# A hybrid decoder layer on one core: the router at four items a head, gates from item 53, 34 more rows in the U half, and a mixer end that adds squares

## The chip, the cores and the metric

One Trainium2 chip, one of its cores. The time is device microseconds (us) of one execution of the whole program; lower is better. The engines are TensorE (PE), VectorE (DVE), ScalarE (ACT), GpSimd (POOL) and SyncE (SP); SP issues most transfers, POOL the indirect ones.

## The reference

One layer over 512 prompt tokens and 32 sample tokens (T = 544), width 1024. What the change touches:

```python
h = h + concat([y_ssd, y_lru]) @ w_out          # the mixer's end, 16 output products
xn = rmsnorm(h, norm_ffn)
q = (xn @ wq).reshape(n, 8 heads, 2 halves, 128)
s_top, i_top = top_k(einsum(q, sub_keys), 16)    # 2 x 128 keys a head
best, pos = top_k(sums of the pairs, 16)         # 16 of 16384 experts a head
g = softmax(best)
act = gelu(einsum(xn, expert_u[idx]))
h = h + einsum(g * act, expert_v[idx])
```

Then a gated embedding and a last rmsnorm. All in float32.

## The kernel before, in words

The program has three stages: the mixer, the experts and the closing. Each engine's instructions are written out in one order; only semaphores tie the engines.

**Mixer.** 51 weight tiles, n = 0 to 50, one product of 48 matmuls each. The last eight (from OS0 = 43) belong to the residual. ssd_add(d) on DVE adds the product to h through tmp, ACT squares h[d] into one of two buffers sq, and PE sums the squares over the partitions with a matmul by ones, sums(3, d). The root of the sum starts the experts' norm. Ahead of that SP spreads rows of decays: the L tiles (1 MB each) and ce (spread_e), which carry(c) on DVE waits for.

**Experts.** 384 prompt tokens (the last three blocks of 128) are dense: all 16384 experts are computed and a gate matrix of 128 x 128 per token masks them. The other 128 prompt tokens and the 32 sample tokens are sparse: their 320 rows of experts are gathered one index per partition, 160 of U (a dot product each) and 160 of V (an addition each).

The order is by items. Items 0 to 143 are the U half: 16 of them are query items (QITEM, 48 matmuls, two per head), 128 are U items (24 matmuls, then a gelu into one of four buffers Ab, which SP stores to acts). Items 144 to 271 are the V half (24 matmuls each). Every item takes a weight tile from a ring of four: SP loads Rw, ACT casts it to Rh, DVE makes the rest Rl. In step n the engines do: PE product n; ACT the evacuation of n, then the cast for n + 4, which waits for product n's end; DVE Rl(n + 4), then its other work of step n; SP, eight ahead, the act store of n and the load of n + 8.

The other work is placed by numbers. A head that starts at item n has its scores behind item n + 3, and topk in six parts from step n + 5 on DVE. After four heads (a group) come, from LOOK[g]: decode, five look-ups (lookup(g, 0) is the sparse prompt block, 1 to 3 the dense ones, in every second step, and lookup(g, NDB) the samples), and softmax in step LOOK[g] + 9. The sparse two and softmax free 80 indices for the gathers (idx); sx tells PE that the dense tokens' numbers (gs) are there. At TURN PE transposes them, turns(). From G0 to GEND 96 gate units stand between the items: one-hot tiles on DVE and ACT, four matmuls on PE, a copy into stg on ACT, and a store of gates by SP for every eight units.

ROWS says how many sparse rows are done by which item; between its points rows are spread evenly. row(r) waits for its gather; POOL has four buffers ug for the gathers.

At GEND SP waits until all gates have landed, then loads Gq (1.5 MB, gates of eight expert rows) and three Aq (acts of four rows, 0.75 MB each). DVE multiplies them (h_full), ACT casts the product to Hh, DVE makes Hl, and item 144 can start. h_hi(0) stands behind the evacuation of item 143 on ACT. In V a new Aq comes every four items and a new Gq every eight, ahead of the next Rw on SP's queue.

Of the kernel before, what the change touches and what calls it, by code (L numbers as in the profile page):

```python
# [9 lines left out]
ALU = mybir.AluOpType  # L10
# [24 lines left out]
NIT = 2 * PH + PK  # L35
HEAD_AT = [0, 6, 12, 18, 34, 40, 46, 52]
LOOK = [29, 63]
QITEM = [n + 2 * s for n in HEAD_AT for s in range(2)]
# [134 lines left out]
def mixer(nc, sh, ring, x, wm, par, head, w_rg, w_ig, conv_in, s0, lru0, ssd_p, ssd_s, conv_o, lru_o):  # L173
# [71 lines left out]
    tmp = at("tmp", A6, [P, T])  # L245
    rstdB = at("rstdB", A6 + 2 * T * 4, [P, T])
    yh = at("yh", A4, [P, ND, T], F32R)
    yl = at("yl", A5, [P, ND, T], F32R)
# [15 lines left out]
    def sync(sp):  # L264
# [8 lines left out]
        def spread_e(c):  # L273
            for g in range(NG):
                spread(ce[g * 64:g * 64 + 64, c % 2, :, :].rearrange("p j l -> p (j l)"),
                       eacd[c, g * HG:(g + 1) * HG, :].rearrange("j l -> (j l)"), 64, "ce%d" % (c // 3))

# [8 lines left out]
        for n in range(2, NW):  # L286
# [26 lines left out]

            if n == 38:
                sp.wait_ge(S("mm"), OL0)
                for c in range(2, 4):
                    spread(L[c][:, :, :].rearrange("p h l -> p (h l)"), acsd[c, :, :].rearrange("h l -> (h l)"), P,
                           "ab%d" % (c // 2))
                sp.wait_ge(S("act_c"), 2 * NXC)
                sp.wait_ge(S("cout_s"), 2 * NXC)  # L320
                spread_e(1)
                spread_e(2)
                sp.dma_start(conv_o, cout[:, :, :]).then_inc(S("out_s"), 16)
# [92 lines left out]
    def tensor(pe):  # L416
# [172 lines left out]
        for n in range(NW):  # L589
# [31 lines left out]
            if n == OS0:  # L621
                pe.wait_ge(S("sad"), 5)
                pe.wait_ge(S("shl"), 3 * ND)
                for k in range(ND):
                    sums(2, k, sq8[:, k, :])
            if n >= OS0 + 2:
                d = n - OS0 - 2
                if d == 0:
                    pe.wait_ge(S("root"), 3)
                sums(3, d, sq[:, d % 2, :])  # L630
        for d in range(ND - 2, ND):
            sums(3, d, sq[:, d % 2, :])

    def scalar(a):
# [88 lines left out]
        for n in range(1, NW + 1):  # L723
# [129 lines left out]
            if n >= OS0 + 2:  # L853
                d = n - OS0 - 2
                a.wait_ge(S("ose"), 2 * (d + 1))
                if d >= 2:
                    a.wait_ge(S("sq_free"), 3 * ND + d - 1)
                square(3, d, sq[:, d % 2, :], h[:, d, :])
        a.wait_ge(S("ose"), 2 * ND)
        a.wait_ge(S("sq_free"), 4 * ND - 2)  # L860
        square(3, ND - 1, sq[:, (ND - 1) % 2, :], h[:, ND - 1, :])
        ring.hi(a, 3)

    def vector(v):
# [109 lines left out]
        def carry(c):  # L974
            v.wait_ge(S("ce%d" % (c // 3)), 64 if c < 3 else 32)
            v.tensor_copy(dec[:, c, :], ce[:, c % 2, :, P - 1:P].rearrange("p j a -> p (j a)")).then_inc(S("cem"), 1)
            v.wait_ge(S("cem"), 2 * c - 1)
            v.tensor_tensor(ce[:, c % 2, :, :], ce[:, c % 2, :, :],
                            xs[:, 9:10, chunk(c)].broadcast_to([P, HG, P]), ALU.mult).then_inc(S("cem"), 1)
# [35 lines left out]
        def ssd_lo(k, part):  # L1015
# [3 lines left out]
            else:  # L1019
                v.wait_ge(S("shl"), 2 * ND + k + 1)  # L1020
                v.wait_ge(S("sq_ready"), 3 * ND)
            v.scalar_tensor_tensor(out=yl[:, k, t], in0=xs[:, k, t], scalar=col("norm_ssd", k),
                                   in1=yh[:, k, t].bitcast(F32), op0=ALU.mult, op1=ALU.subtract).then_inc(S("sll"), 1)

        def sample_add(b):
# [15 lines left out]
        for n in range(1, NW + 1):  # L1041
# [188 lines left out]
            if n >= OS0 + 1:  # L1230
                ssd_add(n - OS0 - 1)
            if n == NW - 1:
                for m in range(3):
                    ring.lo(v, m)
        ring.lo(v, 3)

# [3 lines left out]
def experts(nc, sh, ring, keys, vn, un):  # L1240
# [44 lines left out]
    NALL = NIT + PK  # L1285
    TURN = 77
    G0 = 79
    GEND = 139

# [20 lines left out]

    ROWS = [(46, 0), (78, 36), (VI - 1, 146), (NALL - 5, 2 * IDC)]

# [191 lines left out]
    def scalar(a):  # L1504
# [48 lines left out]
        def h_hi(i):  # L1553
            a.wait_ge(S("hfd"), i + 1)
            need(a, "wmm", VI + 4 * (i - 1) if i >= 2 else 0)
            a.copy(Hh[:, i % 2, :, :], Aq[:, i % 3, :, :]).then_inc(S("hhi"), 1)

        def exps(g):
            a.preload_act_table(ACT.Exp)
            a.wait_ge(S("smx"), g + 1)  # L1560
            a.activation(tu[:, 4, :], tu[:, 4, :], ACT.Exp).then_inc(S("cf"), 1)
            a.preload_act_table(ACT.Gelu_apprx_tanh)
# [5 lines left out]
        for n in range(NIT):  # L1568
# [19 lines left out]
            for j in units(n):  # L1588
                gate_out(j)
            if n == NIT - 1:  # L1590
                h_hi(0)
        for n in range(NIT, NALL):
# [3 lines left out]
            if g % 4 == 1 and g // 4 + 1 < PK // 4:  # L1596
                h_hi(g // 4 + 1)
            if rows_upto(n) >= IDC > rows_upto(n - 1):
                a.wait_ge(S("sdt"), IDC)
                a.activation(coef[:, :], dots[:, :], ACT.Gelu_apprx_tanh).then_inc(S("cf"), 1)  # L1600

    def vector(v):
# [142 lines left out]
        def softmax(g):  # L1745
# [16 lines left out]
            v.sem_inc(S("idx"), 1)  # L1762
            v.sem_inc(S("sx"), 1)

# [41 lines left out]
        for n in range(NALL):  # L1806
            if n + 4 < NALL:
                ring.lo(v, n + 4)
            for part in range(6):
                if head_at(n, 5 + part) is not None:  # L1810
                    topk(head_at(n, 5 + part), part)
            for g in range(2):
                step = n - LOOK[g]
                if step == 0:
                    decode(g)
                if 1 <= step < 9 and step % 2 == 1:
                    lookup(g, step // 2)
                if step == 8:
                    lookup(g, NDB)
                if step == 9:  # L1820
                    softmax(g)
            if n == 0:
                v.wait_ge(S("out_s"), 16 * 3)
# [282 lines left out]
```

## Time and profile before

| | |
|---|---|
| Runs | 1953.18 us median of 3 (1946.73 to 1957.24) |
| The profiled execution | 1952.73 us; span of the trace 1950.6 us |
| PE busy | 1828.0 us, 94% of the span |
| DVE busy | 1461.8 us, 75% |
| ACT, POOL busy | 848.7 us (44%), 514.0 us (26%) |
| Mean granted clock of PE | 0.975 |
| Moved by DMA | 462.63 MB, mean 237 GB/s |

The mixer runs to about 463 us, the U half from 470 to 1226, the V half from 1243 to 1819, the closing to the end. Busy times are of engines, and several engines work at once; a wait of PE is what adds to the time.

### The profile page before, as it was taken

Reading aid. Unit: us, or ns where it says so; the run is one execution under the profiler, and the core shown is the slowest. Engines: PE = TensorE matmul, PEld = TensorE weight load, DVE = VectorE, ACT = ScalarE, POOL = GpSimd, SP = SyncE. Lnnn points to the kernel's source line nnn. Section 1 sums busy time; section 2 is a strip of 40 time slices with the busy share of each in tenths; the row PEclk is TensorE's granted clock in tenths of the full one; section 3 lists DMA queues with packets and bytes.
Section 4 is the critical chain, followed back from the end, with each engine's and each line's share of the span. In section 5 each row is a group of like instructions: output and inputs, shape, how many; then the busy total and the mean of one; then the engine's idle time right before and its main releaser. Section 6 shows DMA issues by size and latency. Waiting matters only on the chain.

```text
span 1950.6 us, 29824 instructions
## 1 busy us (share of the span) xinstructions
PE 1828.0 (94%) x11502; PEld 1756.7 (90%) x11502; DVE 1461.8 (75%) x2584; ACT 848.7 (44%) x1236; POOL 514.0 (26%) x415
## 2 busy tenths in 40 slices
PE   6999989998999999999999999699999999999694
PEld 5999977788999999999999999699999999999693
DVE  4736587556478778999999998588888878788524
ACT  4556672314333333347777776233233323323322
POOL 1200120000000002345444444344445444344000
PEclk9999989998999999999999999899999999999897
DMA  3222333114334447789999999999999999897111
GB/s 128 78 67 85 114 123 99 50 55 166 119 126 157 152 159 237 242 314 343 377 360 351 369 360 354 379 386 359 361 383 379 381 377 359 336 372 264 66 54 46
DMA packets 162616, 462.63 MB, mean 237 GB/s; under 512 B 16496, under 2 KB 74544, under 8 KB 160048
## 3 DMA queue, kind: packets, MB, share of 16 engines
q1 hardware_dynamic: 116400, 292.99, 41.5%
q0 software_dynamic: 46080, 167.79, 23.0%
q8 instruction: 89, 1.46, 0.3%
q14 instruction: 47, 0.39, 0.1%
HBM read 405.46 MB, written 55.27 MB: 236 GB/s over the span
## 4 chain that ended last, share of the span: by engine, by line
PE 69%; DVE 13%; DMA 11%; ACT 3%; issue 2%; SPq 1%; POOL 0%; DVEq 0%; ACTq 0%; POOLq 0%
PE PS L449 11%; DMA Rw<-vn 8%; PE PS L1416 8%; PE PS L1417 8%; PE PS L1418 8%; PE PS L1429 5%; PE PS L1430 5%; PE PS L1431 5%; PE PS L1405 5%; PE PS L1476 4%; PE PS L1898 3%; DVE Hl L1789 2%; PE PS L129 2%; ACT Rh L164 1%; DVE Rl L169 1%
## 5 line engine op out<-in xcount | busy, mean ns | idle before, releaser
L169 DVE TENSOR_TENSOR Rl<-Rw,Rh 128x1024 fp32r<-128x1024 f32 x272 | 332.1, 1222 | 171.2 <-ACT Rh L164 167.7
L164 ACT CAST Rh<-Rw 128x1024 fp32r<-128x1024 f32 x272 | 284.2, 1046 | 389.8 <-PE PS L1431 341.1
L1386 POOL DMA_INDIRECT ug<-un,idxU x160 | 239.2, 1495 | 579.6 <-DVE dots L1797 354.3
L1429 PE MATMUL PS<-Hh,Rh 128*128 128x384 f32 x1024 | 352.2, 344 | 37.1 <-DVE Hl L1789 36.9
L1416 PE MATMUL PS<-Xh,Rh 128*128 128x384 f32 x1024 | 353.9, 346 | 3.8 <-DVE Rl L169 2.7
L1430 PE MATMUL PS<-Hl,Rh 128*128 128x384 f32 x1024 | 349.1, 341 | 0.0
L1431 PE MATMUL PS<-Hh,Rl 128*128 128x384 f32 x1024 | 348.8, 341 | 0.0
L1417 PE MATMUL PS<-Xl,Rh 128*128 128x384 f32 x1024 | 345.0, 337 | 0.0
L1418 PE MATMUL PS<-Xh,Rl 128*128 128x384 f32 x1024 | 344.0, 336 | 0.0
L1386 POOL DMA_INDIRECT ug<-vn,idxU x160 | 232.2, 1451 | 280.2 <-DVE yacc L1802 218.6
L1429 PEld LDWEIGHTS PS<-Hh,Rh 128*128 128x128 f32 x1024 | 194.7, 190 | 46.5 <-issue 46.3
L1416 PEld LDWEIGHTS PS<-Xh,Rh 128*128 128x128 f32 x1024 | 192.6, 188 | 7.3 <-DVE Rl L169 4.6
L1430 PEld LDWEIGHTS PS<-Hl,Rh 128*128 128x128 f32 x1024 | 194.9, 190 | 0.0
L1431 PEld LDWEIGHTS PS<-Hh,Rl 128*128 128x128 f32 x1024 | 194.6, 190 | 0.0
L1417 PEld LDWEIGHTS PS<-Xl,Rh 128*128 128x128 f32 x1024 | 192.6, 188 | 0.0
L1418 PEld LDWEIGHTS PS<-Xh,Rl 128*128 128x128 f32 x1024 | 192.2, 188 | 0.0
L1517 ACT ACTIVATE Ab<-PS 128x384 f32<-128x384 f32 x128 | 62.8, 490 | 267.4 <-PE PS L1418 267.3
L1802 DVE SCALAR_TENSOR_TENSOR yacc<-ug,coef,yacc 128x1024 f32<-128x1024 f32 x128 | 164.4, 1284 | 10.6 <-DMA ug<-vn,idxU 7.3
L1797 DVE CUSTOM_DVE_ANT_0 ug<-ug,xtok 128x1024 f32<-128x1024 f32 x128 | 153.4, 1216 | 14.7 <-DMA ug<-un,idxU 14.4
L870 DVE TENSOR_TENSOR Wlo<-Wr,Whi 128x1024 fp32r<-128x1024 f32 x51 | 62.2, 1221 | 93.7 <-ACT Whi L640 93.7
L449 PE MATMUL PS<-xhi,Whi 128*128 128x272 f32 (+1 forms) x560 | 119.6, 295 | 13.3 <-DVE xlo L885 9.3
L449 PE MATMUL PS<-xhi,Wlo 128*128 128x272 f32 (+1 forms) x560 | 116.9, 291 | 0.0
(378 smaller groups left out, 3074.6 us busy)
## 6 DMA issues: line engine op xcount, KB each, us to landing
Rw<-uw SPq DMA_DIRECT2D x144, 512.0 KB, 4.8
Rw<-vn SPq DMA_DIRECT2D x128, 512.0 KB, 7.9
Wr<-wm SPq DMA_DIRECT2D x51, 512.0 KB, 3.2
acts<-Ab SPq DMA_DIRECT2D x128, 192.0 KB, 5.4
gates<-stg SPq DMA_DIRECT2D x12, 2048.0 KB, 9.8
Gq<-gates SPq DMA_DIRECT2D x16, 1536.0 KB, 12.9
Aq<-acts SPq DMA_DIRECT2D x32, 768.0 KB, 10.3
w_ple_ring<-w_ple SPq DMA_DIRECT2D x8, 640.0 KB, 4.3
```

The lines of the kernel that those rows point to most:

```text
L164: a.copy(self.Rh[:, q, :], self.Rw[:, q, :]).then_inc(self.S("rhi"), 1)
L169: v.tensor_tensor(self.Rl[:, q, :], self.Rw[:, q, :], self.Rh[:, q, :].bitcast(F32), ALU.subtract).then_inc(self.S("rlo"), 1)
L449: r = pe.matmul(pair(s, m)[:, q, :], w_sb[:, s, k, 0:m], x_sb[:, k, q * HT:(q + 1) * HT], start=first, stop=last)
L1386: p.indirect_dma_start(out=ug[:, r % 4, :], out_offset=None, in_=un if r < IDC else vn, in_offset=bass.IndirectOffsetOnAxis(ap=idxU[:, r % ...
L1416: pe.matmul(out, Rh[:, q, w], Xh[:, k, P:NP], start=(k == 0), stop=False)
L1417: pe.matmul(out, Rh[:, q, w], Xl[:, k, P:NP], start=False, stop=False)
L1418: r = pe.matmul(out, Rl[:, q, w], Xh[:, k, P:NP], start=False, stop=(k == ND - 1))
L1429: pe.matmul(out, Rh[:, q, w], hh, start=(g == 0), stop=False)
L1430: pe.matmul(out, Rh[:, q, w], hl, start=False, stop=False)
L1431: r = pe.matmul(out, Rl[:, q, w], hh, start=False, stop=(g == PK - 1))
L1797: v.tensor_tensor_reduce(ug[:, q, :], ug[:, q, :], (xtok if own else xtokS)[:, :], 1.0, 0.0, ALU.mult, ALU.add, dots[:, c:c + 1]).then_inc ...
L1802: v.scalar_tensor_tensor(out=y[:, :], in0=ug[:, q, :], scalar=coef[:, c:c + 1], in1=y[:, :], op0=ALU.mult, op1=ALU.add).then_inc(S("sdt"), 1)
```

## The change

Two edits in the mixer and one set in the experts.

Mixer end: the squares of h[0] to h[6] are no longer summed by PE tile by tile. DVE adds them into sqa (square_add), and PE sums sqa and the last square, two products in place of eight. The square buffers are freed by sqa. And at n = 38 SP issues spread_e(1) ahead of the two L tiles.

Experts: heads stand four items apart, in two runs of four. Parts 0 and 1 of topk, and parts 3 and 4, share a step. Look-ups start with the sparse prompt block and the samples in one step, softmax follows, then one dense block a step; sx moves from softmax to the last look-up. turns() comes at item 51, gates run from item 53 to 131, rows start at item 26. By the end of the U half 180 rows are done instead of 146. The sparse gelu (sparse_act) may now come in the U half.

```diff
-HEAD_AT = [0, 6, 12, 18, 34, 40, 46, 52]
-LOOK = [29, 63]
+HEAD_AT = [0, 4, 8, 12, 24, 28, 32, 36]
+LOOK = [21, 45]
...
+    sqa = at("sqa", A6 + T * 4, [P, T])
...
-                       eacd[c, g * HG:(g + 1) * HG, :].rearrange("j l -> (j l)"), 64, "ce%d" % (c // 3))
+                       eacd[c, g * HG:(g + 1) * HG, :].rearrange("j l -> (j l)"), 64, "ce%d" % (c // 2))
...
             if n == 38:
+                sp.wait_ge(S("act_c"), 2 * NXC)
+                sp.wait_ge(S("cout_s"), 2 * NXC)
+                spread_e(1)
                 sp.wait_ge(S("mm"), OL0)
                 for c in range(2, 4):
...
-                sp.wait_ge(S("act_c"), 2 * NXC)
-                sp.wait_ge(S("cout_s"), 2 * NXC)
-                spread_e(1)
                 spread_e(2)
...
-            if n >= OS0 + 2:
-                d = n - OS0 - 2
-                if d == 0:
-                    pe.wait_ge(S("root"), 3)
-                sums(3, d, sq[:, d % 2, :])
-        for d in range(ND - 2, ND):
-            sums(3, d, sq[:, d % 2, :])
+        pe.wait_ge(S("root"), 3)
+        pe.wait_ge(S("sqa"), ND - 2)
+        for q in range(2):
+            m = pe.matmul(pair(3)[:, q, :], ones[:, :], sqa[:, q * HT:(q + 1) * HT], start=True, stop=False)
+        pe.wait_ge(S("sq_ready"), 4 * ND)
+        for q in range(2):
+            m = pe.matmul(pair(3)[:, q, :], ones[:, :], sq[:, (ND - 1) % 2, q * HT:(q + 1) * HT], start=False,
+                          stop=True)
+        m.then_inc(S("sq_free"), ND)
...
                 if d >= 2:
-                    a.wait_ge(S("sq_free"), 3 * ND + d - 1)
+                    a.wait_ge(S("sqa"), max(1, d - 2))
                 square(3, d, sq[:, d % 2, :], h[:, d, :])
         a.wait_ge(S("ose"), 2 * ND)
-        a.wait_ge(S("sq_free"), 4 * ND - 2)
+        a.wait_ge(S("sqa"), ND - 3)
...
+        def square_add(d):
+            v.wait_ge(S("sq_ready"), 3 * ND + d + 1)
+            if d >= 2:
+                v.wait_ge(S("sqa"), d - 1)
+            v.tensor_tensor(sqa[:, :], sq[:, 0, :] if d == 1 else sqa[:, :], sq[:, d % 2, :], ALU.add
+                            ).then_inc(S("sqa"), 1)
...
                 ssd_add(n - OS0 - 1)
+                if n >= OS0 + 4:
+                    square_add(n - OS0 - 3)
...
+        square_add(ND - 2)
         ring.lo(v, 3)
...
-    TURN = 77
-    G0 = 79
-    GEND = 139
+    TURN = 51
+    G0 = 53
+    GEND = 131
...
-    ROWS = [(46, 0), (78, 36), (VI - 1, 146), (NALL - 5, 2 * IDC)]
+    ROWS = [(25, 0), (53, 30), (GEND, 156), (VI - 1, 180), (NALL - 5, 2 * IDC)]
...
+        def sparse_act(n):
+            if rows_upto(n) >= IDC > rows_upto(n - 1):
+                a.wait_ge(S("sdt"), IDC)
+                a.activation(coef[:, :], dots[:, :], ACT.Gelu_apprx_tanh).then_inc(S("cf"), 1)
...
-            v.sem_inc(S("sx"), 1)
...
-            for part in range(6):
-                if head_at(n, 5 + part) is not None:
-                    topk(head_at(n, 5 + part), part)
+            for part, at in enumerate((5, 5, 6, 7, 7, 8)):
+                if head_at(n, at) is not None:
+                    topk(head_at(n, at), part)
...
-                if 1 <= step < 9 and step % 2 == 1:
-                    lookup(g, step // 2)
-                if step == 8:
+                if step == 1:
+                    lookup(g, 0)
                     lookup(g, NDB)
-                if step == 9:
+                if step == 2:
                     softmax(g)
+                if 3 <= step < 6:
+                    lookup(g, step - 2)
+                if step == 5:
+                    v.wait_ge(tc, ntc[0])
+                    v.sem_inc(S("sx"), 1)
```

The first place is DVE at the end of the second group, the last dense look-up. E, itop, ab and iotaX serve a look-up, gs are the numbers for PE, the line with ug is a sparse row, Boh a one-hot tile of the gates. Before:

```order
L169 TENSOR_TENSOR Rl<-Rw,Rh 128x1024 [waits rhi]
L1725 TENSOR_TENSOR E<-ab,iotaX 128x2048 [waits tc]
L1729 TENSOR_TENSOR E<-E,itop 128x2048 [waits tc]
L1718 TENSOR_TENSOR E<-E 128x2x512 [waits tc]
L1718 TENSOR_TENSOR E<-E 128x2x256 [waits tc]
L1718 TENSOR_TENSOR E<-E 128x2x128 [waits tc]
L1720 TENSOR_TENSOR gs<-E 128x2x64 [waits tc]
L1797 ISA ug,dots<-ug,xtok 128x1024 [waits gt1]
L1797 ISA dots 128x1
L1797 ISA ug,dots<-ug,xtok 128x1024 [waits gt2]
L1797 ISA dots 128x1
L169 TENSOR_TENSOR Rl<-Rw,Rh 128x1024 [waits rhi]
```

After:

```order
L169 TENSOR_TENSOR Rl<-Rw,Rh 128x1024 [waits rhi]
L1742 TENSOR_TENSOR E<-ab,iotaX 128x2048 [waits tc]
L1746 TENSOR_TENSOR E<-E,itop 128x2048 [waits tc]
L1735 TENSOR_TENSOR E<-E 128x2x512 [waits tc]
L1735 TENSOR_TENSOR E<-E 128x2x256 [waits tc]
L1735 TENSOR_TENSOR E<-E 128x2x128 [waits tc]
L1737 TENSOR_TENSOR gs<-E 128x2x64 [waits tc]
L1813 ISA ug,dots<-ug,xtok 128x1024 [waits tc,gt1]
L1813 ISA dots 128x1
L169 TENSOR_TENSOR Rl<-Rw,Rh 128x1024 [waits rhi]
L1791 TENSOR_TENSOR Boh<-iota,ijg 128x1024 [waits gtc]
L1785 TENSOR_SCALAR Aoh<-iota,ijg 128x128 x6
```

Before, seven Rl, six rows at least, the samples' look-up and softmax stand between this look-up and Boh; after, one row and one Rl do, and the samples' look-up and softmax have gone ahead.

The second place is SP around the last gates store (gw is its landing, glu an Ab that is ready, gev a stg). Before:

```order
L1330 DMA acts<-Ab 128x384 [waits glu]
L1334 DMA gates<-stg 128x4096 [waits gev]
L157 DMA Rw<-vn 128x1024 [waits rlo,rhi]
L1345 DMA Gq_179<-gates 128x12x256 [waits gw1,gw0]
L1340 DMA Aq<-acts 128x4x384 [waits as2,as3,as1,as0] x3
L1330 DMA acts<-Ab 128x384 [waits glu]
L157 DMA Rw<-vn 128x1024 [waits rlo,rhi]
L1330 DMA acts<-Ab 128x384 [waits glu]
L157 DMA Rw<-vn 128x1024 [waits rlo,rhi]
```

After:

```order
L1343 DMA acts<-Ab 128x384 [waits glu]
L1347 DMA gates<-stg 128x4096 [waits gev]
L157 DMA Rw<-uw 128x1024 [waits rlo,rhi]
L1358 DMA Gq_180<-gates 128x12x256 [waits gw1,gw0]
L1353 DMA Aq<-acts 128x4x384 [waits as2,as3,as1,as0] x3
L1343 DMA acts<-Ab 128x384 [waits glu]
L157 DMA Rw<-uw 128x1024 [waits rlo,rhi]
L1343 DMA acts<-Ab 128x384 [waits glu]
L157 DMA Rw<-uw 128x1024 [waits rlo,rhi]
```

The same wait for gates and the same four loads stand in it, but now Rw of the U half (uw) and act stores with U items to come are queued behind them.

## Rows read from the trace of the kernel before

**Rows 1.** The page: span, DMA share in 40 slices, two groups, one issue.
```profile
span 1950.6 us, 29824 instructions
...
DMA  3222333114334447789999999999999999897111
...
L169 DVE TENSOR_TENSOR Rl<-Rw,Rh 128x1024 fp32r<-128x1024 f32 x272 | 332.1, 1222 | 171.2 <-ACT Rh L164 167.7
L164 ACT CAST Rh<-Rw 128x1024 fp32r<-128x1024 f32 x272 | 284.2, 1046 | 389.8 <-PE PS L1431 341.1
...
acts<-Ab SPq DMA_DIRECT2D x128, 192.0 KB, 5.4
```

**Rows 2.** Waits of PE, whole span: us in total, times, longest.
```profile
PE PS L1429 <- DVE Hl L1789: 36.9, 15, 17.1
...
PE PS L1416 <- DVE Rl L169: 2.7, 3, 1.4
PE PS L1416 <- ACT Ab L1517: 0.8, 1, 0.8
PE PS L516 <- DVE ST L963: 0.4, 1, 0.4
```

**Rows 3.** Windows by stage: busy us (instructions) by engine, granted clock, DMA, GB/s.
```profile
540.50:572.20 31.70, 31.70 (x215) 31.06 (x214) 21.98 (x108) 10.42 (x16) 0.00 (x0) 1.00 0.37 125
594.00:644.00 50.00, 50.00 (x286) 50.00 (x286) 42.24 (x180) 20.30 (x29) 0.00 (x0) 1.00 0.49 157
772.90:855.30 82.40, 78.64 (x441) 76.73 (x440) 80.63 (x230) 28.73 (x39) 28.20 (x18) 1.00 0.74 250
870.00:1208.00 338.00, 338.00 (x2203) 337.80 (x2202) 317.28 (x601) 255.83 (x406) 154.28 (x103) 1.00 0.96 359
1208.00:1226.00 18.00, 18.00 (x106) 17.72 (x104) 10.29 (x16) 6.75 (x9) 6.10 (x6) 1.00 1.00 393
1243.00:1819.00 576.00, 555.89 (x3082) 546.74 (x3082) 471.25 (x387) 173.32 (x156) 251.09 (x173) 0.98 0.93 351
1669.00:1675.00 6.00, 2.02 (x12) 1.69 (x10) 2.97 (x3) 2.09 (x2) 0.00 (x0) 0.90 0.73 295
1675.00:1682.00 7.00, 6.93 (x25) 6.97 (x26) 4.77 (x4) 0.00 (x0) 3.80 (x3) 0.60 0.87 301
```

**Rows 4.** Waits in V, 1243 to 1819: ACT cast for the ring.
```profile
ACT Rh L164 <- DMA Rw<-vn: 46.2, 16, 5.9
```

**Rows 5.** Timeline of SP around the last gates store: start, us, issue.
```profile
1210.82 0.32 SPq L1334 DMA_DIRECT2D gates<-stg  x1
...
1231.04 1.77 SPq L1330 DMA_DIRECT2D acts<-Ab  x1
```

**Rows 6.** DMA issues from 1230 to 1232: last number, us to landing.
```profile
acts<-Ab SPq DMA_DIRECT2D x1, 192.0 KB, 9.6
```

**Rows 7.** Chain that ended last, 1206 to 1262: start, us, what.
```profile
1210.82 11.26 DMA gates<-stg
...
1222.68 13.49 DMA Aq<-acts
...
1241.38 1.68 DVE Hl L1789
...
1244.57 13.86 DMA Rw<-vn
```

**Rows 8.** DVE groups, 1213 to 1226: busy, mean ns, idle before.
```profile
L1797 DVE CUSTOM_DVE_ANT_0 ug<-ug,xtok 128x1024 f32<-128x1024 f32 x4 | 4.9, 1225 | 4.9 <-DMA ug<-un,idxU 4.9
```

**Rows 9.** Chain that ended last, end of the mixer.
```profile
452.92 0.92 PE PS L479 x4
...
459.89 0.74 DVE tmp L1006
...
461.41 0.66 ACT sq L697
...
463.03 1.22 DVE Rl L169
```

More of the change, by code:

```diff
@@ L974, in carry @@
         def carry(c):
-            v.wait_ge(S("ce%d" % (c // 3)), 64 if c < 3 else 32)
+            v.wait_ge(S("ce%d" % (c // 2)), 32 if c < 3 else 64)
             v.tensor_copy(dec[:, c, :], ce[:, c % 2, :, P - 1:P].rearrange("p j a -> p (j a)")).then_inc(S("cem"), 1)
@@ L1589, in scalar @@
                 gate_out(j)
+            sparse_act(n)
             if n == NIT - 1:
@@ L1597, in scalar @@
                 h_hi(g // 4 + 1)
-            if rows_upto(n) >= IDC > rows_upto(n - 1):
-                a.wait_ge(S("sdt"), IDC)
-                a.activation(coef[:, :], dots[:, :], ACT.Gelu_apprx_tanh).then_inc(S("cf"), 1)
+            sparse_act(n)
     def vector(v):
```

## The prediction

> **What bounds the kernel now.** I read the page, then the waits of TensorE (PE), then windows by stage. The page puts the profiled execution at a span of 1950.6 us [rows 1]; the execution took 1952.73 us, 2.1 us more, which I add at the end. The median of the runs shown is 1953.18, so both stand for the same kernel. A measurement of this kernel tells about 0.5% (9.8 us) from no change: faster means under 1943.4, slower over 1962.9.
>
> PE is the bound nearly everywhere; what it waits for is what an edit can win or lose. The reader is to see three places in [rows 2]. The largest is Hl: 36.9 us in 15 waits, of which 17.1 us is one wait, at the junction of the U and V halves. The other 14 (19.8 us) lie inside V. In the router part PE waits 2.7 us for Rl and 0.8 us for Ab. Everything else in the U half is PE's own work: an ungated product item has 24 matmuls, and 286 of them fill 50.0 us, so an item is 4.2 us [rows 3].
>
> The second resource is DMA. From 870 us on it is 0.96 busy, and saturated it moved 393 GB/s [rows 3]; the page's DMA row reads 9 from the 19th slice to the 34th [rows 1]. In V the ring cast waited 46.2 us, 16 times, for a late Rw [rows 4], and these late Rw stand behind Gq and Aq on SP's queue: one took 13.86 us to land [rows 7].
>
> VectorE (DVE) is third. It makes Rl(n+4) in step n, after product n has ended, so its usual lead is three items minus a cast (1.05) and an Rl (1.22) [rows 1]: 12.6 - 2.3 = 10.3 us. More lag than that and PE waits.
>
> **The change, part by part.**
>
> Mixer end. Between the last output products stood sums over sq, 0.92 us each [rows 9]. Five of them lay ahead of the last product's end: 4.6 us of PE go. The end gets longer: after the last product come tmp (0.74), h, then square_add(5) (about 0.7, like the DVE operation on the same 128x544 tile beside it), since the last square now waits for it, then the square (0.66), and behind the squares ring.hi(3) and ring.lo(3) (1.22) [rows 9]. I put 1.2 us on that tail: net -3.4. Bounds: 0 (the tail takes it all) and -4.6. spread_e(1) ahead of the L loads: PE's wait behind that path is the 0.4 us for ST [rows 2]; DVE had other work meanwhile. -0.4. Together **-3.8**.
>
> Router, closer heads. One head of four blocks: six items take 31.7 us, DVE busy 21.98, of which six Rl (1.22 each, [rows 1]) are 7.3; so a head costs DVE 14.7 us [rows 3]. At four items a head PE's period is 31.7 - 2 x 4.2 = 23.3. DVE needs 14.7 + 4 x 1.22 = 19.6 in heads 0 to 3, which fits. In heads 4 to 7 about 4.3 rows come along (1.22 each alone [rows 8], some 1.15 from start to start in a row of them): 24.5. It falls behind by 1.2 us a head, 3.6 over three, about 4 when the last head's search begins.
>
> Router, the second group's end. This is the largest term. Before, DVE needed 82.4 us from step 57 (last head's search, five blocks) to the end of step 72 (softmax) [rows 3]. In it are 16 Rl (19.5) and 18 rows (20.7; the gathers on POOL are 18 too); 42.2 us are search, decode, five look-ups and softmax. PE took 16 items meanwhile, 67 us: DVE used up its lead, and that made the 3.5 us of waits. After, the same 42.2 us stand in steps 41 to 50, with 10 Rl (12.2) and 9 rows (10.4): 64.8 us. And the transposes of turns(), now behind item 51, wait for sx, which comes at the end of step 50's look-up. From product 41's end PE has ten items to there, 42.0 us. DVE starts 1.3 after that product, 4 late: 64.8 + 1.3 + 4 - 42.0 = **+28** us of waiting. It doesn't all show at sx: Rl, and ACT, which stands in exps(1) for decode while Ab is late, take some 11 of it first, and sx some 17. The 3.5 of before go (**-3.5**). Bounds: +23 (no lag brought along) and +31. An item behind the wait is slower: after the 4 us gap that ended at 1675 (PE busy 2.02 of 6 us) the granted clock was 0.60 for 7 us, 2.8 us lost [rows 3]; I take **+1.5**.
>
> Gates from 53. 96 units over 79 items instead of 61. PE and DVE have the same instructions, thinner, and DVE was at 317 of 338 us without making PE wait [rows 3]. Nothing.
>
> The junction. Before, the last gates store was issued at 1210.82 with four items left, landed 11.26 us later, then Aq took 13.49, then the product of Gq and Aq, Hh and Hl: the 17.1 us [rows 5, 7]. After, it stands twelve items ahead, 50 us, and the chain of 32 us fits. What stays is ACT's order: h_hi(0) stands behind u_out(143) and the ring's cast. From PE's last U matmul: Ab and its handover 0.7, cast 1.05 [rows 1], Hh some 1.5 and Hl 1.68 [rows 7] on the same size of tile, and handovers: 5.4 us. **-11.7**. Bounds: -9 and -13. The first V item stays slow, as now.
>
> The tail of U. SP now waits for the gates store with products left to feed. By [rows 5] the next act store was issued 20.2 us behind the gates store, and it landed in 9.6 [rows 6]: 29.8. u_out(136) needs that store (four buffers Ab), item 138 needs u_out(136), and item 138 would start some 23 us behind the gates store: 7 us of waiting. And more is moved: 2 rows an item instead of 1.7, into the same window as Gq and three Aq. From the gates store to V: gates 2.1 MB, Gq and Aq 3.9, nine Rw 4.7, act stores 2.0, 22 rows 11.5, 24.2 MB; at 393 GB/s that is 62 us, where the nominal way takes 54 (twelve items less the 2 us already gone, and 5.4). Rows are held back meanwhile: the trace shows four in 13 us, 4.9 us idle for them [rows 8]. I take **+11**, and **+1.8** for the clock behind it. Bounds: 0 and +22.
>
> V. 34 rows fewer, 17.8 MB. Over eight items SP needs Gq, two Aq and eight Rw, 7.3 MB; rows 11.2 x 0.524 = 5.9: 13.2 MB in 34.2 us is 386 GB/s, as much as there is. After, 12.0 MB: 353. A late Rw has 2.9 MB ahead of and with it and took about 14 us; with 25 of some 200 GB/s more for SP it lands 1.5 us sooner. 14 waits share 19.8 us; each 1.5 shorter, none below zero, leaves about 6. **-14**, and **-3.5** for the slow stretches behind the longer ones. Bounds: 0 and -24.
>
> A rule on this: the Trainium skill, page "DMA: Bandwidth & Descriptors", section "Queues, rings and completion order", says that each engine takes turns between the queues that have work, a packet at a time. By it a late Rw shares with the gathers half and half while any gather is in flight, however many rows follow; V would gain nothing. It is the first rival's ground.
>
> Sum: -3.8 - 3.5 + 28 + 1.5 - 11.7 + 11 + 1.8 - 14 - 3.5 = +5.8; 1950.6 + 5.8 + 2.1 = 1958.5. **The change moves some 35 us of waiting from V and the junction into the U half.** I say 1958.
>
> **The rivals.**
>
> 1. Slower: V gains nothing (0.22). In a burst the gathers' share is set by what is in flight, up to four, not by the quota. For it: [rows 8], and that V as a whole ran at 351 GB/s and still had its longest wait at 1675 [rows 3]. Against: then the DMA engines would idle more between bursts, and a burst would meet no backlog. Time: 1958 + 17.5 = 1975. It is slower by the bound from 5 us of lost gain on.
> 2. Faster: the tail costs nothing, since rows only lag (DVE's lead is 10 us) and Ab's store lands in the median 5.4 [rows 1] instead of 9.6, and V's waits vanish (0.19). Time: 1958 - 12.8 - 7 = 1938.
> 3. Faster: the 28 us come back. While PE waits at sx, DVE and the queues catch up, and what they are ahead by saves as much in the tail and in V (0.06). Against: their lead is four items at most, and the tail comes 80 items later. Time: 1958 - 28 = 1930.
> 4. The forecast, a small loss or none, 1944 to 1967 (0.53).
>
> **How the numbers follow.** The forecast's own range is 1944 to 1967; to hold 8 in 10 it goes to 1938 and to 1974. Faster by over 0.5%: rivals 2 and 3 without their edges, 0.22. Slower: rival 1 and the upper end of the forecast, 0.31. Within: 0.47.
>
> **What would show it.** Right: a wait of PE for sx (a DVE look-up, gs) of 12 to 20 us, and waits for Rl and Ab before it, 28 us together; the junction's wait 5 to 7 us; a wait for Ab of 6 to 12 us six items behind the last gates; V's waits at 3 to 9 us; the last sums of the mixer 3 us sooner. Wrong: PE idle under 10 us around the turns would break the largest term, V's waits still near 20 would give rival 1, and no wait in the tail rival 2.

## The result, and the profile after

The changed kernel takes 1962.39 us (median of 8 runs, 1961.38 to 1967.14); the kernel before, in runs beside it, 1954.63 (8 runs, 1946.73 to 1958.83). The ratio is 1.0051, 95% interval 1.003 to 1.0071: a loss of some 8 to 10 us, just at the bound of what I called the same. The profiled execution has a span of 1962.7 us, 12.1 more than [rows 1]: it is 2 us above its median, and the profiled one of before is 2 below, so the account below is of 12 us and not of 8. Its page, with the busy tenths of PE, the granted clock and DMA in 40 slices:

```profile
span 1962.7 us, 29787 instructions
...
PE   6999989997999985999999999599999999999694
...
PEclk9999989998999998999999999899999999999898
DMA  3222332124335655899999999999999999996111
```

PE's row before the change was:

```profile
PE   6999989998999999999999999699999999999694
```

After the change the row has one new dent, at the 16th slice (the turns, 5, with an 8 ahead of it); the one at the 26th (the end of the U half and the junction) was there and is a little deeper, 5 for 6. The DMA row reads 9 from the 18th slice to the 36th, where [rows 1] has 9 from the 19th to the 34th: the heavy traffic starts a slice sooner. The waits of PE (us in total, times, longest), which answer to [rows 2]:

```profile
PE PS L1478 <- DVEq L1841: 15.4, 1, 15.4
PE PS L1429 <- ACT Ab L1530: 15.4, 3, 11.9
...
PE PS L1442 <- DVE Hl L1805: 11.3, 1, 11.3
PE PS L1429 <- DVE Rl L169: 9.3, 4, 3.7
...
PE PS L630 <- DVE sqa L1032: 3.1, 1, 3.1
...
PE PS L517 <- DVE ST L966: 0.7, 1, 0.7
```

The wait for sx (a DVE semaphore instruction, line 1841) is new, Ab has grown from 0.8 to 15.4, Rl from 2.7 to 9.3, and Hl has gone from 36.9 in 15 waits to a single one of 11.3. By windows, as in [rows 3]; the stretches are the last sums of the mixer, the last heads with the turns, the wait near the end of U, the items behind it, and V:

```profile
459.00:463.00 4.00, 3.76 (x8) 2.49 (x8) 1.22 (x1) 0.92 (x2) 0.00 (x0) 0.57 0.00 0
716.00:788.00 72.00, 44.86 (x228) 42.84 (x228) 63.86 (x194) 18.59 (x31) 16.82 (x10) 0.86 0.55 184
...
1229.00:1241.00 12.00, 0.23 (x1) 0.26 (x2) 0.01 (x1) 0.49 (x1) 1.76 (x2) 0.70 1.04 414
1241.00:1250.00 9.00, 9.00 (x44) 9.00 (x45) 7.37 (x7) 3.92 (x5) 4.00 (x3) 0.83 0.86 277
...
1279.10:1830.30 551.20, 551.10 (x3082) 542.00 (x3082) 430.50 (x335) 173.20 (x155) 199.73 (x139) 0.99 0.90 334
```

V's 3082 matmuls take 551.2 us, where [rows 3] has 3082 in 576.0, at 334 GB/s in place of 351. The account of the 12.1 us, from the first and last products of each stage: the U half starts 0.6 sooner (469.50 for 470.12), lasts 42.4 longer (798.3 for 755.9), the wait at the junction is 5.8 shorter (11.3 for 17.1), V lasts 24.6 less (551.2 for 575.8), the closing is 0.8 longer. Of the 42.4 us in U, 27.1 are waits around the turns (before: 3.4 in their place), 13.0 are two waits for Ab near the end, and 5.7 are left. Nearly all of that is the same work done slower. The U half before and after the change, in this order:

```profile
470.12:1226.05 755.93, 751.79 (x4793) 743.69 (x4793) 640.19 (x1744) 403.85 (x628) 215.29 (x145) 1.00 0.73 266
```
```profile
469.50:1267.80 798.30, 757.25 (x4793) 748.31 (x4793) 678.11 (x1795) 404.50 (x629) 264.23 (x178) 0.98 0.77 279
```

The same 4793 matmuls keep PE busy 5.5 us longer, at a granted clock of 0.98 for 1.00. The clock fell to 0.86 over 716 to 788, where before had 1.00 in its windows of the router [rows 3], and to 0.83 behind the wait near the end of U.

The mixer's end, from the chain that ended last (start, us, what), to be read beside [rows 9]:

```profile
455.91 0.74 DVE tmp L1009
...
458.13 0.73 DVE sqa L1032
...
459.00 2.15 PE PS L630 x4
461.15 1.62 PE PS L633 x4
```

The last product now ends 4.0 us sooner (455.88 for 459.85), but then PE waits 3.1 us for sqa, since square_add(5) and square_add(6) stand behind the last tmp and h, and its eight matmuls take 2.15 and 1.62 us at a granted clock of 0.57; the four in [rows 9] took 0.92.

SP around the last gates store (start, us, issue), which answers to [rows 5], and the landing of the act store (last number), which answers to [rows 6]:

```profile
1203.92 0.32 SPq L1347 DMA_DIRECT2D gates<-stg  x1
...
1214.81 0.37 SPq L1358 DMA_DIRECT2D Gq<-gates  x1
1215.34 10.06 SPq L1353 DMA_DIRECT2D Aq<-acts  x3
1225.45 3.43 SPq L1343 DMA_DIRECT2D acts<-Ab  x1
1228.99 1.28 SPq L157 DMA_DIRECT2D Rw<-uw  x1
```
```profile
acts<-Ab SPq DMA_DIRECT2D x1, 192.0 KB, 14.6
```

The act store is issued 21.5 us behind the gates store and lands 14.6 us later: 36.1 us. PE waits 11.89 us for its buffer, to 1240.77. And the end of that half, from the chain that ended last:

```profile
1260.28 9.17 DMA ug<-vn,idxU
...
1271.81 1.75 DVE Aq L1798
...
1277.19 1.76 DVE Hl L1805
```

The product of Gq and Aq (line 1798) starts at 1271.81, 4 us after PE's last U matmul ended at 1267.8, since the four rows of the two steps before it stand ahead of it on DVE, and the last of their gathers took 9.17 us to land. Between the end of the product (1273.56) and Hl (1277.19) DVE does two more rows and an Rl, 3.6 us.

### The profile page after: what moved, and what is told of

The parts are those of the page before. It is cut to its first block, busy times and chain, and to the rows that moved or that the text cites. A ratio compares the mean times of both kernels' runs of the same rounds, so it can differ in the third digit from the quotient of the medians.

```text
span 1962.7 us, 29787 instructions
## 1 busy us (share of the span) xinstructions
PE 1826.1 (93%) x11478; PEld 1754.4 (89%) x11478; DVE 1465.3 (75%) x2590; ACT 849.5 (43%) x1236; POOL 513.1 (26%) x415
## 4 chain that ended last, share of the span: by engine, by line
PE 75%; DVE 17%; ACT 2%; DMA 2%; issue 2%; SPq 1%; POOL 0%; DVEq 0%; ACTq 0%; POOLq 0%
PE PS L450 11%; PE PS L1442 10%; PE PS L1444 9%; PE PS L1443 9%; PE PS L1429 7%; PE PS L1430 6%; PE PS L1431 6%; PE PS L1489 4%; PE PS L1918 3%; PE PS L1418 2%; DVE Rl L169 2%; PE PS L129 2%; DVE ug L1813 1%; DVE ctmp L882 1%; PE PS L544 1%
## 5 line engine op out<-in xcount | busy, mean ns | idle before, releaser
L1429 PE MATMUL PS<-Xh,Rh 128*128 128x384 f32 x1024 | 357.2, 349 | 24.7 <-ACT Ab L1530 15.4
L1442 PE MATMUL PS<-Hh,Rh 128*128 128x384 f32 x1024 | 350.2, 342 | 11.4 <-DVE Hl L1805 11.3
## 6 DMA issues: line engine op xcount, KB each, us to landing
Gq<-gates SPq DMA_DIRECT2D x16, 1536.0 KB, 11.9
```

The lines of the kernel that those rows point to most:

```text
L1429: pe.matmul(out, Rh[:, q, w], Xh[:, k, P:NP], start=(k == 0), stop=False)
L1442: pe.matmul(out, Rh[:, q, w], hh, start=(g == 0), stop=False)
```

## The experiments

Theory 1, mine: each wait has the place and cause that the prediction gives it, so each can be taken away or brought back alone: the turns' place makes the wait for sx, SP's wait for the gates the one near the end of U, the number of rows in V the late Rw, the late squares the mixer's. Theory 2, the rival: PE is short of DVE's time or of DMA bandwidth as a whole, and a wait taken away comes back at the next place, so that undoing one part gives nothing. Each kernel was timed against the one before the change.

**The turns and gates six items later.** Heads, look-ups and rows stay.

```diff
-    TURN = 51
-    G0 = 53
+    TURN = 57
+    G0 = 59
```

> The changed kernel with the turns at item 57 instead of 51 and the first gates at 59 instead of 53, all else the same. Theory 1 (the wait for sx is a loss of its own: the transposes stand ten items behind a search that DVE needs fifteen items for): the wait for sx, 15.4 us in the changed kernel, goes; two or three waits for Rl behind it add some 3 us, and the slow stretch after the long wait goes too. 12 to 14 us are won: 1948 to 1951 us. Theory 2 (PE's wait at sx lets DVE and the transfers catch up, and is paid back later): the waits for Rl, for Ab in the tail and for Hl at the junction grow by as much, 0 to 4 us are won: 1958 to 1963.

1953.05 us (1950.41 to 1955.65), ratio 1.0003 [0.9988, 1.0018]. Waits of PE:

```profile
PE PS L1429 <- DVE Rl L169: 12.3, 7, 3.7
PE PS L1442 <- DVE Hl L1805: 12.2, 2, 10.4
PE PS L1429 <- ACT Ab L1530: 11.9, 3, 10.2
```

The wait for sx is gone and Rl grew by 3.0 us only; the time is 2 us above the range of theory 1 and 5 below that of theory 2. In this profile the U half is 13.2 us shorter (785.1) and V keeps its gain (552.1). Of the 27.1 us, 13.2 stay: Rl, and Ab behind them. So 14 us of the largest term hung on the place of the turns alone, against theory 2, and they did not return later: near the end of U the waits for Ab are 11.0 us for 13.0, the junction's is 10.4 for 11.3, and V has one of 1.8 where it had none. The third rival (the 28 us come back) needed them to.

**Loads for V later.** SP waits for the gates three items later, and the three Aq come one an item, not in a block.

```diff
-            if n == GEND:
+            if n == GEND + 3:
                 sp.wait_ge(S("gw0"), 16 * ((NGB + 1) // 2))
                 sp.wait_ge(S("gw1"), 16 * (NGB // 2))
                 load_g(0)
-                for i in range(3):
-                    load_a(i)
+            if GEND + 5 <= n < GEND + 8:
+                load_a(n - GEND - 5)
```

> The changed kernel, but SP waits for the gates and loads Gq three items later than GEND, and the three Aq one an item from five items behind GEND, instead of all four at once at GEND. The same bytes are moved in the same order of queues. Theory 1 (the tail's 13.0 us of waits for Ab come from SP standing in its wait for the gates with act stores queued behind it): they fall under 3 us, the junction's wait for Hl stays near 11 or falls a little: 1949 to 1953 us. Theory 2 (the tail is short of DMA capacity, 24 MB in 54 us): the waits reappear as late rows and late Rl, or at the junction, and less than 5 us are won: 1958 to 1962.

1956.78 us (1954.67 to 1958.1), ratio 1.0012 [0.9998, 1.0025].

```profile
PE PS L1442 <- DVE Hl L1805: 16.1, 2, 15.8
...
PE PS L1429 <- ACT Ab L1530: 3.0, 2, 2.4
```

The time lies between the ranges of the two theories, 4 us above that of theory 1. The waits for Ab near the end fall from 13.0 to 0.6 us, so they came with SP's block; but the junction's goes from 11.3 to 15.8. U takes 785.2 us, 13.1 less, and in this profile 4.5 of them are given to the junction: here theory 2 has a part, a third of the gain. What ends the junction's wait is another thing now. The product of Gq and Aq is done at 1263.5, but Hh stands on ACT behind the ring's last cast, and that waits to 1267.4 for an Rw that took 15.1 us to land. V is 550.8.

**Rows back to those of before.** 134 rows by item 131 and 146 by the end of U.

```diff
-    ROWS = [(25, 0), (53, 30), (GEND, 156), (VI - 1, 180), (NALL - 5, 2 * IDC)]
+    ROWS = [(25, 0), (53, 30), (GEND, 134), (VI - 1, 146), (NALL - 5, 2 * IDC)]
```

> The changed kernel with 146 rows done by the end of the U half, as before the change (134 by item 131, 12 more to 143), instead of 180. Theory 1 (V's waits for Hl went because V gathers 34 rows fewer): V takes some 576 us again instead of 554 with 15 to 20 us of waits; the tail's 13.0 and the junction's 11.3 us shrink by 6 to 10 together, since half as many rows are gathered there: 1970 to 1980 us. Theory 2 (V's waits went because V starts with its queues in another phase, or with more loaded ahead): V keeps its 554 us, and only the tail's and the junction's gain is seen: 1952 to 1957.

1969.42 us (1966.99 to 1976.13), ratio 1.0084 [1.0055, 1.0113]. Waits in V, with the junction's 4.8 us in the first, of PE and of ACT's ring cast:

```profile
PE PS L1442 <- DVE Hl L1805: 22.5, 13, 4.8
```
```profile
ACT Rh L164 <- DMA Rw<-vn: 37.2, 13, 4.6
```

V takes 571.9 us again, with 17.7 us of waits for Hl, and the cast waits 37.2 us for Rw ([rows 4]: 46.2); in the changed kernel it waits for none in V. So the 34 rows are 20.7 of the 24.6 us of V's gain, as theory 1 has it (the time is 0.6 us under its range). The junction falls to 4.8 us with one row an item ahead of it, and the waits for Ab near the end of U fall from 13.0 to 5.9: together 13.6 us, where 6 to 10 were expected. With SP's block as it was, the wait for Ab now ends 29.6 us behind the gates store instead of 36.9. So SP's block and the rows beside it share that wait.

**Mixer's end.** The sixth square's addition goes ahead of ssd_add, h[6] is summed by PE from its own buffer.

```diff
-        pe.wait_ge(S("sqa"), ND - 2)
+        pe.wait_ge(S("sqa"), ND - 3)
...
+        pe.wait_ge(S("sq_ready"), 4 * ND - 1)
+        for q in range(2):
+            m = pe.matmul(pair(3)[:, q, :], ones[:, :], sq[:, 0, q * HT:(q + 1) * HT], start=False, stop=False)
...
-                ssd_add(n - OS0 - 1)
                 if n >= OS0 + 4:
                     square_add(n - OS0 - 3)
+                ssd_add(n - OS0 - 1)
...
-        square_add(ND - 2)
```

> The changed kernel, but only the squares of h[0] to h[5] are added on DVE, each addition ahead of the last residual additions of its step, and PE sums sqa, the square of h[6] and that of h[7] in three products. Theory 1 (the mixer's end got longer because PE waits 3.1 us for sqa behind the last product and then runs its sums at half the clock): PE has no wait over 0.5 us for sqa, the sums take 0.9 to 1.2 us each, and the root starts 2 to 3 us sooner behind the last product (6.9 us in the changed kernel): 1959 to 1961 us. Theory 2 (the end is bound by the chain h, square, root on ACT and DVE, whatever PE does): under 1 us is won: 1962.

1959.61 us (1955.97 to 1961.48), ratio 1.0024 [1.0006, 1.0042]. The chain at the mixer's end:

```profile
456.37 0.73 DVE tmp L1012
...
457.89 0.66 ACT sq L703
...
460.73 3.47 DVE rstd_f L1623
```

It is as theory 1 has it: tmp, h and the square follow each other, PE's wait for sqa is gone, and the router starts at 466.6, 2.9 us sooner than in the changed kernel and 3.5 sooner than before. This kernel also shows how far the junction varies with nothing changed near it: its wait is 7.9 us here for 11.3, with the same two rows an item; the product of Gq and Aq started 0.6 us behind the last U matmul, not 4.0.

**The three together** (turns and gates, loads, mixer).

> The three edits that won alone, together: turns at 57 and gates from 59, SP's loads of Gq and Aq apart from each other, and the mixer's end with three sums. They lie in three places, and their alone-measured gains against the changed kernel are 9, 6 and 3 us. Theory 1 (separate losses): they add up, 1942 to 1947 us, under the kernel before by 0.4%. Theory 2 (each wait taken away lets the next one grow, in the end at the junction, since the tail's rows are late for want of DMA): some 1952 us, as the kernel before.

1942.46 us (1939.16 to 1944.3), ratio 0.9941 [0.9923, 0.996]. From the changed kernel that is 20 us; alone they gave 9, 6 and 3 by the medians. That is 18 of 20, and they add up within the spread of the runs. From item 1 to the end of V no wait is over 4 us but the junction's, 16.5 us. The chain that ended last goes through a late Rw there, as with the loads alone:

```profile
1236.84 15.74 DMA Rw<-vn
...
1252.60 1.04 ACT Rh L164
1253.64 1.38 ACT Hh L1571
```

The product of Gq and Aq had been done 4.4 us before Hh began.

**Ten rows of the last twelve items back to V.** The three, and:

```diff
-    ROWS = [(25, 0), (53, 30), (GEND, 156), (VI - 1, 180), (NALL - 5, 2 * IDC)]
+    ROWS = [(25, 0), (53, 30), (GEND, 156), (VI - 1, 170), (NALL - 5, 2 * IDC)]
```

> The three edits together, and 170 rows by the end of the U half instead of 180, all ten taken from the last twelve items (14 rows in them, not 24). Theory 1 (the junction's wait for Hl of 11 to 16 us is that of rows whose gathers are late, two an item; V needs fewer than 30 of the 34 rows taken from it): the wait falls to 5 to 8 us, which is ACT's order; V's waits stay under 4 us: 1936 to 1941 us. Theory 2 (the junction's wait is that of Aq's transfers behind the products, whatever rows there are, and V is at the edge with 180): the wait stays over 10 us and V's waits come back: 1945 to 1952.

1933.11 us (1930.37 to 1936.04), ratio 0.9893 [0.9863, 0.9923]. The junction's wait falls from 16.5 to 7.3 us and V goes from 550.7 to 552.6 with two waits, 1.4 us in all. The time is 3 us under the range of theory 1. The Rw on the same chain took 11.9 us to land, not 15.7. So ten rows fewer in the last items take away most of the junction's excess (by way of less crowded transfers, it seems, since DVE's part was done before Hh began in both), and V has room for them. By the profiles the junction is 7.3 to 8.6 us in the four versions with 170 rows and 7.9 to 16.5 in the six that do 24 rows in the last twelve items.

**No rows from item 41 to 50**, all else as in the changed kernel:

```diff
-    ROWS = [(25, 0), (53, 30), (GEND, 156), (VI - 1, 180), (NALL - 5, 2 * IDC)]
+    ROWS = [(25, 0), (40, 16), (50, 16), (53, 20), (GEND, 156), (VI - 1, 180), (NALL - 5, 2 * IDC)]
```

> The changed kernel with no rows in steps 41 to 50 (nine rows, 10.3 us of DVE, stood between the last head's search and sx); they are done under the gates. All else as in the changed kernel. Theory 1 (PE waits at the router's end for the sum of DVE's work from step 41 to sx): the waits for Rl, Ab and sx, 27.1 us together in the changed kernel, become 15 to 18, 10 us less: 1951 to 1953 us. Theory 2 (the end is set by the chain of small dependent DVE operations, or by ACT in exps, and rows fill its gaps): the waits stay over 24 us: 1960 to 1962.

1956.49 us (1952.83 to 1961.03), ratio 1.0019 [1.0, 1.0038].

```profile
PE PS L1442 <- DVE Hl L1805: 16.2, 2, 15.5
...
PE PS L1478 <- DVEq L1841: 13.5, 1, 13.5
...
PE PS L1429 <- ACT Ab L1530: 11.8, 3, 8.4
...
PE PS L1429 <- DVE Rl L169: 4.8, 4, 1.4
```

Around the turns PE waits 19.6 us (sx 13.5, Rl 4.8, Ab 1.3) for 27.1: the rows made 7.5. Theory 1 said 15 to 18 and 1951 to 1953 us, so it has the direction and three quarters of the size; that the look-ups, search and softmax make the rest is not shown by a run of its own. The ten rows moved behind item 53 cost PE 0.5 us under the gates (Aoh), but the junction's wait is 15.5 here: in this profile, of 10.8 us that the U half gained, 4.2 went there, about what the junction varies by itself.

**Rows held back and look-ups apart**, singly and together, on the version with 170 rows. Held back: `(40, 16), (53, 20)` in ROWS in place of `(53, 30)`. Apart:

```diff
-                if 3 <= step < 6:
-                    lookup(g, step - 2)
-                if step == 5:
+                if step in (3, 5, 7):
+                    lookup(g, (step - 1) // 2)
+                if step == 7:
```

Both together:

> As the kernel with 170 rows, and the router's groups eased: the three dense look-ups in every second step (sx in LOOK + 7, the turns at 57 stay behind it), and only 4 rows in steps 41 to 53 instead of 14, which are done later under the gates. Theory 1 (what is left at the router's end, 12 to 13 us of waits for Rl, is DVE's work above its lead): DVE has 11 us less to do in these steps, the waits fall under 4 us and nothing grows under the gates, where DVE was 88% busy: 1927 to 1933 us. Theory 2 (rows moved under the gates find the DMA engines full, 0.96 busy): the gates' stretch shows waits for Rl or Ab of 5 us and more: 1936 to 1942.

1930.61 us (1921.76 to 1933.7), ratio 0.9883 [0.9853, 0.9913]. The time is as theory 1 said, the waits are not: Rl and Ab take 8.8 us, where under 4 were expected. The profiled execution is its fastest, span 1920.0, 9 us under the median, and the next is at 1927.64: what its profile shows is not typical of this version. Look-ups apart alone:

> e6_all_rows170 with the dense look-ups of a group in steps 3, 5 and 7 in place of 3, 4 and 5, rows as in e6. e7_spaced had this and fewer rows under the heads; in its trace PE's waits between 716 and 788 us are 9.5 us against 13.2 in e6, and the granted clock there stayed at 1.00 where e6 shows 0.79 to 1.00 (0.91 over 700 to 780). Theory 1, rows under the last heads make those waits: they stay near 13 us here and the clock still falls below 1.00; span within 2 us of e6's 1932.5. Theory 2, three look-ups in a row make them: the wait of 3.7 us at 753 us goes, the clock stays at 1.00, and the U half is some 8 to 10 us shorter than e6's 772.0.

1931.82 us (1928.72 to 1932.88), ratio 0.9891 [0.9867, 0.9915]. Rows held back alone:

> e6_all_rows170 with ROWS at 16 rows by item 40 and 20 by item 53 in place of 30 by 53; look-ups as in e6. Theory 1, rows under the last heads make the waits between 716 and 788 us: they fall from 13.2 to some 9 us, the longest under 2.5, the clock stays at 1.00, and the U half takes some 762 us as in e7_spaced, 10 less than e6. Theory 2, the look-ups in a row make them: the wait of 3.7 us at 753 us stays and the U half is at 768 or more. If neither alone gives e7's 761.8 us, both are needed, and the clock is what ties them: it falls behind waits of about 2 us and more and not behind shorter ones.

1926.55 us (1923.97 to 1930.2), ratio 0.9865 [0.9841, 0.989]. The windows 716 to 788 of the version with 170 rows, and of the one with 170 rows and rows held back (PE, PEld, DVE, ACT, POOL busy, clock, DMA, GB/s):

```profile
716.00:788.00 72.00, 58.80 (x289) 56.26 (x289) 68.79 (x180) 20.02 (x27) 23.33 (x15) 0.91 0.61 209
```
```profile
716.00:788.00 72.00, 62.91 (x343) 60.65 (x344) 64.14 (x165) 24.21 (x38) 13.58 (x9) 0.98 0.62 216
```

Waits of PE there, in the same order:

```profile
PE PS L1431 <- DVE Rl L169: 12.3, 7, 3.7
...
PE PS L1431 <- ACT Ab L1532: 0.9, 1, 0.9
```
```profile
PE PS L1431 <- DVE Rl L169: 7.4, 6, 2.3
PE PS L1431 <- ACT Ab L1532: 2.4, 1, 2.4
```

With look-ups apart alone, PE still waits 12.2 us for Rl and 2.4 for Ab before 800 us, the 3.7 us wait among them: the three look-ups in a row don't make it. The clock there is 0.98 all the same. With rows held back the wait is 9.8 us, the clock 0.98 for 0.91, and item 54 starts 295.0 us after item 0, as with both (294.7), in place of 303.0. So the rows make this part. But the U half as a whole gained only 2.1 us in that profile (769.9 for 772.0), so the 762 us expected did not come: by item 126 the lead is down from 8.0 to 2.1. Some of it went to new waits under the gates, where now 1.74 rows an item have to be done instead of 1.62; the window 1100 to 1150 of that kernel:

```profile
1100.00:1150.00 50.00, 47.90 (x292) 47.39 (x291) 43.99 (x82) 31.95 (x50) 24.50 (x16) 0.97 0.94 336
```

With both edits the profile shows no such loss (U 761.8 us), though rows are placed alike; but that is the execution 9 us under its median, so it doesn't tell the versions apart, and what decides it isn't settled. The intervals of these four versions against the kernel before overlap. Of the two single edits, which were timed side by side, rows held back is the faster by 5 us (five of its six runs are under the fastest with look-ups apart); the rest of the order isn't settled. All four beat the kernel before by about 1%, the best by 1.35% [1.1, 1.6].

## Why the prediction was right, and where not

The time of 1962.39 us lies in the forecast's own range, 4 us above 1958; "a small loss or none" held, and so did the sentence that waiting moves from V and the junction into the U half. The number owes something to luck: as the terms below show, their errors come to some 14 us one way and 8 the other. Of the signs named beforehand, the junction's wait (5 to 7 us) and V's waits (3 to 9) did not come: they are 11.3 and 0. Term by term:

- **Mixer end, -3.8: measured about -0.6.** The five sums went (the last product ends 4.0 us sooner), but the tail was put at 1.2 us and grew by 3.4: from the last product to the root 6.9 us for 3.5. I counted square_add(5) and forgot that square_add(6) stands behind it, and that PE, which waits 3.1 us for it, makes its last eight matmuls at a clock of 0.57. spread_e gave nothing: ST waited 0.4 before and 0.7 after.
- **Second group's end, +28: right.** The waits are 27.1 us in all: 15.4 at sx ("some 17") and 11.7 at Rl and Ab ("some 11"). The count of DVE work against ten items of PE holds for the sum. Its term for the rows (10.4 us) was tested: nine rows fewer gave 7.5.
- **Clock, +1.5 and +1.8: 5.7 measured as what U's waits don't explain, 5.5 of it longer busy time of PE.** Right in kind, too small: not only the long waits lower the clock; it was 0.79 in 724 to 732 and 756 to 764 too, behind waits of 2.5 (with one of 2.05 seven us before it) and 3.7 us.
- **Gates from 53, nothing: right.** PE is busy 330.0 of the 330 us from 870 to 1200.
- **Tail, +11: 13.0.** The wait for Ab is 11.9 us (said: 6 to 12) at item 138, as foreseen. Gates store to act store's landing took 36.1 us for 29.8: the store landed in 14.6 us, not 9.6. The rows beside it have a part in that: with one row an item the same stretch is 7 us shorter and the waits for Ab are 5.9 us.
- **Junction, -11.7: -5.8.** The step that failed is "what stays is ACT's order". ACT was free from 1269.25 to 1273.59; h_full(0) on DVE came late, behind rows that waited for gathers, and Hl stood behind two more rows and an Rl. With one row an item the wait is 4.8 us, so the 5.4 holds for a junction without those rows. With ten rows fewer it is 7.3, on another chain (a late Rw); and with nothing changed there it was 7.9 once, so the size of this error is known to some 3 us only.
- **V, -17.5: -24.6.** The waits gave 19.8 us and PE's busy time 4.8 (551.1 for 555.9, the -3.5). The term that was mis-sized is the waits': I took 1.5 us off each late Rw and left 6 us of waits. (The 25 GB/s behind it is less than the 33 by which the sum's own 386 and 353 differ, and nothing says where the rest goes.) All of them went, though the median landing of Rw in V fell only from 7.9 us to 6.7, the row below: as I read it, the late ones were those of crowded moments, and these are what fewer rows remove.

The transfers issued in V of the changed kernel (last number, median us to landing):

```profile
Rw<-vn SPq DMA_DIRECT2D x122, 512.0 KB, 6.7
...
ug<-vn,idxU POOLq DMA_INDIRECT x139, 7.5
```

The errors of the junction (+5.9), mixer (+3.2), clock (+2.4) and tail (+2.0) were partly paid by V (-7.1); with the router (-0.9) and the closing (+0.8) that is +6.3, what lies between the span of 1956.4 that the sum gave and 1962.7.

**Rival 1** (V gains nothing) fell: V lost its waits with 34 rows fewer and has them again with the rows of before. The rule of the Trainium skill on which it stood (page "DMA: Bandwidth & Descriptors", section "Queues, rings and completion order") isn't touched: no run here shows packets taking turns. What fell is my use of it, that in a crowded moment the number of rows doesn't matter. **Rival 2** was right on V and wrong on the tail: the act store landed in 14.6 us, not the median 5.4. **Rival 3** fell with the turns six items later, where 14 us less of waiting cost at most 1.8 later, in V.

## What to carry to other kernels

When a hand-written order is drawn together, count for the engine that feeds PE what must be done between two fixed places, and set the consumer behind it: six items of delay for the turns gave back 9 us and cost next to nothing. A blocking wait on a queue that still feeds the main loop is paid by the buffers behind it, so issue each transfer when it can go, one an item; and move bulk work out of a stretch that is just at its bandwidth, but not into the last items before a hand-over. Look at the chain again after each edit: the junction's wait kept its name (Hl) while its cause went from late rows on DVE to a late weight tile on ACT. Undo the parts of a mixed change singly: here V's 24.6 us were a gain, hidden under costs of which 20 us came off with three small edits, and with ten rows given back to V and ten held back in the router the kernel was 1.35% faster than before, where the whole change had lost 0.5%.

## What the runs showed of the hardware that was not expected

- After 3.1 us of idleness two groups of four matmuls took 2.15 and 1.62 us at a granted clock of 0.57, where such a group takes 0.92 [rows 9]. Where PE idled 0.43 us ahead of the last group, it took 1.19 us in the timeline, as before the change (1.18). So here a short idle ahead of a short piece on the path about doubled that piece.
- The clock doesn't follow from the length of one wait. Behind waits of 2.06 us (at 719.6, with 170 rows) the granted clock in 716 to 724 was 0.79; behind one of 2.80 at the same place, with look-ups apart, it was 1.00, the two rows below in this order. So the guess of the last expectation, a bound at waits of about 2 us, doesn't hold. What decides it stays open.

```profile
716.00:724.00 8.00, 5.94 (x25) 5.62 (x25) 7.97 (x42) 1.42 (x2) 1.68 (x1) 0.79 0.44 147
```
```profile
716.00:724.00 8.00, 5.01 (x28) 4.37 (x26) 7.97 (x41) 1.69 (x3) 1.68 (x1) 1.00 0.48 157
```

- DMA traffic had an edge rather than a slope: V at 351 GB/s [rows 3] had 14 waits and 19.8 us of them, with 170 rows done before it, ten more in V than in the changed kernel, 342 GB/s and two waits, 1.4 us in all, and at 334 GB/s none. With 146 rows it was 352 GB/s and 17.7 us again. The other kernels with 180 rows show up to 1.8 us in one wait, so in these runs the edge is between 342 and 351 GB/s, and nothing finer is known.
